# Seven block products for the second input half of the second feed-forward parts

## The reference

```python
def swiglu(x, w_in, w_out):                     # w_in 1024 x 5632, w_out 2816 x 1024
    gate, up = jnp.split(x @ w_in, 2, axis=-1)
    return (jax.nn.silu(gate) * up) @ w_out
x = x + 0.5 * swiglu(rmsnorm(x, p['ffn2_norm'][i]), p['ffn2_w_in'][i], p['ffn2_w_out'][i])
```

## Time and profile before

| | us |
|---|---|
| median of 3 runs (2357.9 to 2358.71) | 2358.68 |
| profiled execution, span from first to last instruction | 2357.9 |
| PE busy | 2332.7 (99%) |
| DVE busy | 1295.9 (55%) |
| ACT busy | 869.0 (37%) |
| POOL busy | 609.4 (26%) |

### The profile page before, as it was taken

The page is one execution under the profiler, slowest core; times in us unless marked ns, Lnnn a source line. Parts: engine busy times, 40 slices in busy tenths (PEclk is TensorE's granted clock), DMA queues, the critical chain, the costliest instruction groups (busy, mean ns, idle before and its releaser), DMA issues.

```text
span 2357.9 us, 50146 instructions
## 1 busy us (share of the span) xinstructions
PE 2332.7 (99%) x21043; PEld 2270.3 (96%) x21043; DVE 1295.9 (55%) x1906; ACT 869.0 (37%) x1399; POOL 609.4 (26%) x591
## 2 busy tenths in 40 slices
PE   8999999999999999999999999999999999999999
PEld 8999999889979999999999999999999979999999
DVE  6653643964576443445543344577777666443443
ACT  4422333453233321322433233267775233321323
POOL 4779967331103000004111010432122102000003
PEclk9999999999999999999999999999999999999999
DMA  6455445553562333333543333233332653333332
GB/s 167 128 161 149 123 134 169 171 170 107 166 242 84 98 99 91 96 96 99 158 117 111 100 108 115 83 100 108 104 111 77 213 188 91 97 94 94 98 94 94
DMA packets 483707, 289.19 MB, mean 123 GB/s; under 512 B 22289, under 2 KB 466962, under 8 KB 482514
## 3 DMA queue, kind: packets, MB, share of 16 engines
q1 hardware_dynamic: 477856, 280.66, 40.4%
q0 software_dynamic: 560, 1.84, 0.6%
q10 hardware_dynamic: 5122, 4.25, 0.5%
HBM read 258.86 MB, written 27.85 MB: 122 GB/s over the span
## 4 chain that ended last, share of the span: by engine, by line
PE 90%; DVE 4%; POOL 2%; ACT 1%; issue 1%; DMA 1%; SPq 0%; DVEq 0%; POOLq 0%; ACTq 0%
PE lin L3021 51%; PE lin L3026 25%; PE mis L2512 4%; POOL sTmp L737 1%; PE mis L2650 1%; PE lin L2600 1%; PE lin L2762 1%; PE mis L2633 1%; PE lin L2757 1%; PE lin L2983 1%; POOL sGe L738 0%; DVE w_lo L1827 0%; POOL sFe L738 0%; PE lin L2650 0%; PE mis L2626 0%
## 5 line engine op out<-in xcount | busy, mean ns | idle before, releaser
L1827 DVE TENSOR_TENSOR w_lo<-raw,w_hi 128x1024 fp32r<-128x1024 f32 (+1 forms) x322 | 464.0, 1441 | 294.4 <-ACT w_hi L1330 293.7
L1330 ACT ACTIVATE w_hi<-raw 128x1024 fp32r<-128x1024 f32 (+1 forms) x328 | 365.1, 1113 | 314.2 <-PE lin L3026 244.4
L3021 PE MATMUL lin<-a_rear,w_hi 128*128 128x264 f32 x3552 | 455.6, 279 | 0.0
L3021 PE MATMUL lin<-a_front,w_hi 128*128 128x256 f32 x3552 | 451.5, 279 | 1.1 <-DVE a_rear L1840 0.7
L3021 PEld LDWEIGHTS lin<-a_rear,w_hi 128*128 128x128 f32 x3552 | 432.6, 188 | 0.0
L3021 PEld LDWEIGHTS lin<-a_front,w_hi 128*128 128x128 f32 x3552 | 424.4, 188 | 4.5 <-issue 1.8
L3026 PE MATMUL lin<-a_rear,w_lo 128*128 128x264 f32 x1776 | 245.1, 278 | 0.0
L3026 PE MATMUL lin<-a_front,w_lo 128*128 128x256 f32 x1776 | 240.5, 277 | 1.0 <-DVE w_lo L1827 1.0
L2391 DVE SCALAR_TENSOR_TENSOR xT<-lin,xT 128x520 f32<-128x520 f32 (+1 forms) x87 | 60.9, 700 | 322.8 <-PE lin L3026 322.1
L1063 POOL TENSOR_TENSOR acc<-xT 128x520 f32<-128x520 f32 x8 | 12.2, 1521 | 864.6 <-DVE xT L2391 836.6
L3026 PEld LDWEIGHTS lin<-a_rear,w_lo 128*128 128x128 f32 x1776 | 223.8, 188 | 0.0
(11 more groups left out here) (512 smaller groups left out, 3181.5 us busy)
## 6 DMA issues: line engine op xcount, KB each, us to landing
raw<-in_ffn_w_in_dram SPq DMA_DIRECT2D x176, 512.0 KB, 3.9
raw<-in_ffn_w_out_dram SPq DMA_DIRECT2D x64, 704.0 KB, 4.6
kc<-in_cache_mem_k_dram SPq DMA_DIRECT2D x32, 512.0 KB, 7.1
vc<-in_cache_mem_v_dram SPq DMA_DIRECT2D x16, 1024.0 KB, 9.1
raw<-in_hg_w_in_dram SPq DMA_DIRECT2D x32, 512.0 KB, 4.3
raw<-in_xattn_w_kv_dram SPq DMA_DIRECT2D x16, 512.0 KB, 4.4
raw<-in_s_w_glu_dram SPq DMA_DIRECT2D x16, 512.0 KB, 4.0
raw<-in_xattn_w_q_dram SPq DMA_DIRECT2D x16, 512.0 KB, 3.9
```

Of the source, the lines that this page charges most:

```text
L1330: act.activation(w_hi[:, j, 0:kt, :], raw[:, j, 0:kt, :], ACT.Copy).then_inc(hi_ready, 1)
L1827: dve.tensor_tensor(low_weights(n, j), raw[:, j, 0:kt, :], w_hi[:, j, 0:kt, :].bitcast(F32), ALU.subtract).then_inc(lo_ready, 1)
L3021: pe.matmul(lpart(j, half), high[:, k, :], (x_lo if u else x_hi)[half][:, k, :], start=start and u == 0 and k == 0, stop=False)
```

## The change

`ffn2_in1` of both layers (2 x 11 pairs) is computed by Winograd's form of Strassen's scheme. The 2x2 blocks are: weights A11, A12 (gate, tiles 0 to 3 and 4 to 7 of the contraction), A21, A22 (value); tokens B11, B21 (the first 260 tokens, tiles 0 to 3 and 4 to 7), B12, B22 (the last 260). Per pair there are seven products P1 to P7 of 4 tiles x 3 matmuls with 260 columns, 84 matmuls:

- P1 = A11 B11, P2 = A12 B21, P4 = A22 T4, P6 = S2 T2, P5 = S1 T1, P7 = S3 T3, P3 = S4 B22, in this order on PE, each in a PSUM bank of its own.
- S1 = A21+A22, S2 = S1-A11, S3 = A11-A21, S4 = A12-S2, four sums of 128x512 per pair on DVE (`weight_sums`); their high parts on ACT (`high_sums`, two of 128x1024), their low parts on POOL (`low_sums`, two of 128x1024, of which the first waits for S4 too).
- Normalised token blocks and T1 to T4 (four steps of eight DVE ops with 260 columns, `mixed`), their high parts on ACT and low parts on DVE (128x1820 each), made in `ffn2_in0`, which is now unrolled.
- The results are put together on DVE from PSUM and `rows` (`with_p2_p6`, `with_p5_p7`, `with_p3_p4`), then silu, product and split as before.

SP's code is unchanged, but in `ffn2_in1` `lo_ready` is raised only by `low_22`, by 2; the low part of the gate's weights raises `first_low`. At the end of `ffn2_out0` DVE makes the first pair's sums before it adds the last tile to x. Two hgrn semaphores are merged, and `rows_in` shrinks from 8 to 4 semaphores.

```diff
+    COMBOS = {"B11": 0, "B22": 1, "B21": 2, "T1": 3, "T2": 4, "T3": 5, "T4": 6}
...
+    SUMS = {"S1": 0, "S2": 1, "S3": 2, "S4": 3}
...
+    MIX_RAW = {("ffn2_in0", l, 1 + 2 * k): k for l in range(DEPTH) for k in range(KQ)}
+    MIX_SPLIT = {("ffn2_in0", l, 2 + 2 * k): k for l in range(DEPTH) for k in range(KQ)}
...
+            def low_sums(layer):
+                for q in range(FH * layer, FH * (layer + 1)):
+                    pool.wait_ge(combined, of_weights(q, 1))
+                    for pair in range(2):
+                        pool.wait_ge(combined_high, of_weights(q, pair))
+                        blocks = slice(2 * pair, 2 * pair + 2)
+                        pool.tensor_tensor(sum_lo[:, q % FH % 2, blocks], sum_raw[:, q % FH % 2, blocks],
+                                           sum_hi[:, q % FH % 2, blocks].bitcast(F32), ALU.subtract).then_inc(combined_low, 1)
...
+                def high_22(p):
+                    act.wait_ge(raw_arrived[1], 16 * (p + 1))
+                    act.wait_ge(chunk_done, 2 * p0)
+                    wait(act, product_done, 4 * (FH * layer + p - p0 - 1) + 2)
+                    act.activation(w_hi[:, 1, KQ:KD, :], raw[:, 1, KQ:KD, :], ACT.Copy).then_inc(hi_ready, 1)
+                def high_sums(q, pair):
+                    act.wait_ge(combined, of_weights(q, pair))
+                    blocks = slice(2 * pair, 2 * pair + 2)
+                    act.activation(sum_hi[:, q % FH % 2, blocks], sum_raw[:, q % FH % 2, blocks], ACT.Copy)\
+                        .then_inc(combined_high, 1)
...
+                for i in range(FH):
+                    p, q, more = p0 + i, FH * layer + i, i + 1 < FH
+                    if i == 0:
+                        high_sums(q, 0)
+                        high_22(p)
+                        high_sums(q, 1)
+                    else:
+                        gate(i - 1)
+                    act.wait_ge(product_done, 4 * q + 1)
+                    act.activation(rows[:, ROW_P1], bank_p1, ACT.Copy).then_inc(product_kept, 1)
+                    if more:
+                        high_sums(q + 1, 0)
+                    split(p + 1, 0, n if more else n + 1)
+                    if i:
+                        hidden_hi(i - 1)
+                    if more:
+                        high_22(p + 1)
+                        high_sums(q + 1, 1)
...
+            def weight_sums(p, q, pair):
+                for j in range(2):
+                    dve.wait_ge(raw_arrived[j], 16 * (p + 1))
+                s = {name: sum_raw[:, q % FH % 2, b] for name, b in SUMS.items()}
+                w = {f"A{j + 1}{e + 1}": raw[:, j, KQ * e:KQ * (e + 1), :] for j in range(2) for e in range(2)}
+                if pair == 0:
+                    step.link(dve.tensor_tensor(s["S1"], w["A21"], w["A22"], ALU.add))
+                    dve.tensor_tensor(s["S2"], s["S1"], w["A11"], ALU.subtract).then_inc(combined, 1)
+                else:
+                    dve.tensor_tensor(s["S3"], w["A11"], w["A21"], ALU.subtract)
+                    dve.wait_ge(combined, of_weights(q, 0))
+                    dve.tensor_tensor(s["S4"], w["A12"], s["S2"], ALU.subtract).then_inc(combined, 1)
...
                                 split_part(p + 1, slice(0, FREE_LOW)).then_inc(lo_part, 1)
+                                if seven(n + 1):
+                                    weight_sums(p + 1, FH * layer, 0)
+                                    weight_sums(p + 1, FH * layer, 1)
...
+                            if last and j == 1 and seven(n + 1):
+                                split_part(p + 1, slice(FREE_LOW, KD)).then_inc(first_low, 1)
...
+                def low_11(p):
+                    dve.wait_ge(hi_ready, 2 * p + 1)
+                    dve.tensor_tensor(w_lo8[:, 0], raw[:, 0, 0:KD, :], w_hi[:, 0, 0:KD, :].bitcast(F32),
+                                      ALU.subtract).then_inc(first_low, 1)
+                def low_22(p):
+                    dve.wait_ge(hi_ready, 2 * p + 2)
+                    dve.tensor_tensor(w_lo8[:, 1, KQ:KD, :], raw[:, 1, KQ:KD, :], w_hi[:, 1, KQ:KD, :].bitcast(F32),
+                                      ALU.subtract).then_inc(lo_ready, 2)
...
+                def with_p2_p6(q):
+                    dve.wait_ge(product_done, 4 * q + 3)
+                    dve.wait_ge(product_kept, q + 1)
+                    return step.mark(dve.tensor_tensor(rows[:, ROW_GATE.stop - 1:ROW_U2 + 1:ROW_U2 - ROW_GATE.stop + 1],
+                                                       banks_p2_p6, twice(ROW_P1), ALU.add))
+                def with_p5_p7(q, u2):
+                    dve.wait_ge(product_done, 4 * q + 4)
+                    step.after(u2)
+                    step.link(dve.tensor_tensor(rows[:, ROW_V:ROW_U3 + 1], banks_p5_p7, twice(ROW_U2), ALU.add))
+                    dve.tensor_tensor(rows[:, ROW_VALUE.start], bank_p5, rows[:, ROW_U3], ALU.add)
+                def with_p3_p4(p):
+                    dve.wait_ge(chunk_done, 2 * p + 2)
+                    dve.tensor_tensor(rows[:, ROW_GATE.start:ROW_VALUE.stop:ROW_VALUE.stop - 1 - ROW_GATE.start], banks_p3_p4,
+                                      rows[:, ROW_V:ROW_U3 + 1], ALU.add).then_inc(used[0], 1)
...
+                for i in range(FH):
+                    p, q, more = p0 + i, FH * layer + i, i + 1 < FH
+                    if i == 0:
+                        low_22(p)
+                    else:
+                        with_p3_p4(p - 1)
+                    if more:
+                        weight_sums(p + 1, q + 1, 0)
+                    if i:
+                        gated(i - 1)
+                    if more:
+                        weight_sums(p + 1, q + 1, 1)
+                        low_11(p + 1)
+                    u2 = with_p2_p6(q)
+                    if more:
+                        low_22(p + 1)
+                    else:
+                        split(p + 1, 0, n + 1)
+                    if i:
+                        hidden_lo(i - 1)
+                    with_p5_p7(q, u2)
+                with_p3_p4(p)
+                gated(FH - 1)
+                hidden_lo(FH - 1)
...
+                def high(bank, w, block):
+                    for x in (mix_hi, mix_lo):
+                        for k in range(KQ):
+                            pe.matmul(bank, w[:, k, :], x[:, COMBOS[block], k, :],
+                                      start=x is mix_hi and k == 0, stop=False)
+                def low(bank, w, block):
+                    for k in range(KQ):
+                        ins = pe.matmul(bank, w[:, k, :], mix_hi[:, COMBOS[block], k, :], start=False,
+                                        stop=k == KQ - 1)
+                    return ins
+                pe.wait_ge(combined_low, of_tokens(layer, KQ - 1))
+                for i in range(FH):
+                    p, q = p0 + i, FH * layer + i
+                    a1_hi, a1_lo = w_hi[:, 0], w_lo8[:, 0]
+                    s_hi, s_lo = ({name: t[:, i % 2, b] for name, b in SUMS.items()} for t in (sum_hi, sum_lo))
+                    pe.wait_ge(hi_ready, 2 * p + 1)
+                    wait(pe, product_kept, q)
+                    high(bank_p1, a1_hi[:, 0:KQ], "B11")
+                    if i == 0:
+                        pe.wait_ge(lo_part, LOW_PARTS.index(n) + 1)
+                    else:
+                        pe.wait_ge(first_low, q + 1)
+                    low(bank_p1, a1_lo[:, 0:KQ], "B11").then_inc(product_done, 1)
+                    if i:
+                        pe.wait_ge(lo_ready, 2 * p + 2)
+                    pe.wait_ge(used[0], p - 1)
+                    high(bank_p2, a1_hi[:, KQ:KD], "B21")
+                    if i == 0:
+                        pe.wait_ge(first_low, q + 1)
+                    low(bank_p2, a1_lo[:, KQ:KD], "B21").then_inc(chunk_done, 1)
...
+                    pe.wait_ge(hi_ready, 2 * p + 2)
+                    pe.wait_ge(used[0], p)
+                    high(bank_p4, w_hi[:, 1, KQ:KD], "T4")
+                    pe.wait_ge(lo_ready, 2 * p + 2)
+                    low(bank_p4, w_lo8[:, 1, KQ:KD], "T4").then_inc(product_done, 1)
+                    pe.wait_ge(combined_high, of_weights(q, 0))
+                    high(bank_p6, s_hi["S2"], "T2")
+                    pe.wait_ge(combined_low, of_weights(q, 0))
+                    low(bank_p6, s_lo["S2"], "T2").then_inc(product_done, 1)
```

More of the change, by code:

```diff
@@ L55, in link, with mark, after @@
         self.eng.wait_ge(self.sem, self.off + self.n)
+    def mark(self, ins):
+        ins.then_inc(self.sem, 1)
+        self.n += 1
+        return self.off + self.n
+    def after(self, mark):
+        self.eng.wait_ge(self.sem, mark)
     def loop(self, i, first, per):
@@ L451, in trunk_kernel @@
     hg = {name: sem("hg_" + name) for name in
-          ("fill", "void_dve", "void_act", "lb_diff", "lb_exp", "lb", "consts", "log", "decay", "exps", "scaled_pool",
```

(63 more changed lines are left out.)

70 lines of the change are left out of this document (64 added, 6 removed).

## The result

The changed kernel takes **2460.7 us** (median of 4 runs, 2458.55 to 2461.67) against 2358.55 of the kernel before (4 runs on the same chip). That is 1.0431 times, 95% interval 1.0416 to 1.0446. The forecast was 2459. The profiled execution took 2460.23, its span is 2458.5. The page after, answering to the earlier trace rows: engines' busy time, the granted clock in 40 slices, the chain that ended last.

What follows compares the result with a forecast made beforehand. PE bounds the kernel before (99% busy); a closed loop of loads, DVE and POOL would bound the changed stretches: 4.9+10x15.7+9.4 = 171.3 us against 121.7, so 2357.9+99+2 = 2459 us, range 2380 to 2480.

Steps and rivals of the forecast that it cites:

- PE would no longer bound: Changed stretches: a pair's 84 matmuls need 9.66 us, but the loop sets the turn; PE busy near 60%.
- The loop: ffn2_in1, low_22 through both loads, sums and low_11 to the next low_22: 12.0 us a turn alone; as rival 2386, chance 0.11.
- The port, POOL first: SBUF port shared with DVE: POOL's low part starts about 0.1 us before low_11, turn 15.7 us; chance 0.52.
- the other order: Rival at the port: low_11 goes before POOL, turn 13.5 us, 2421 us; chance 0.25 including turns of both kinds.
- Entry: Start of each changed stretch: first low_22 ends at 943.05, 4.9 us after PE's start.
- The last pair: End of each changed stretch: P2, then P4 after with_p3_p4, then five products of 1.38, 9.4 us.
- P6's slack: PE in a turn: P6 has 7 us of slack, so a clock fall for part of a pair costs nothing.
- clock rival: PE in the changed stretches: lower clock throughout, 19.3 us a pair, two stretches +182, 2541 us; chance 0.05.
- The first input half: ffn2_in0, unrolled with added DVE and ACT work: +2 us, ends 0 and +8.
- The faster rival: Changed stretches: loads overlap enough that PE bounds at 9.66 us a pair, 2330 us; chance 0.07.
- 14.3+10T: Time of one changed stretch, T being one turn of the loop; breaks even with 121.7 us at T = 10.7.

Runs made afterwards that it cites:

- run 2: Changed kernel with POOL's low parts of the sums cut to 8 of 1024 columns from each layer's third pair, part of the computation left out: 2390.28 us.
- run 3: Changed kernel with both low parts of the sums made on DVE behind low_22 instead of on POOL: 2387.32 us.
- Run 4: As run 3, but SP loads raw[:,0] once low_11 has read it, not low_22: 2370.77 us.
- Run 1: Changed kernel with POOL's first low part of a pair's sums let go only behind low_11: 2427.6 us.
- Run 10: Order of run 8, with POOL's low part held until the moved hidden_lo is done: 2343.84 us, 0.993 of the kernel before.
- run 8: Version with DVE's sums, low_11, low_22 first and POOL keeping one low part; hidden_lo of the pair before moved behind low_22: 2371.63 us.

## Why the prediction was right

- **PE would no longer bound**: 84 matmuls a pair and a stretch of 172.05 us, PE busy 135 of it, 78% where the forecast had near 60%. At 119 ns the 924 matmuls are 110 us, 64%. The rest is mostly the lower clock: PE was busy 10.77 us in the turn from 1020.41, with a granted clock of 0.99, and 13.20 in that from 958.02, with 0.81.
- **The loop.** Forecast 12.0 us without POOL; 11.85 in run 2, 11.82 in run 3. The 5.7 us of the two loads came out as 0.6+5.1. Run 4 took one release out of the loop and 16.6 us out of the time.
- **The port, POOL first.** Forecast 15.7 a turn; 15.49 on average (`low_22` ends at 942.89 in the first turn and at 1097.81 ten turns later). POOL started 0.07 us after S4's end, not 0.15, so its lead over `low_11` was 0.18 instead of 0.1. Run 1 showed what hung on it: forecast 13.5 and 2421 for the other order, measured 13.75 and 2427.6.
- **Entry**: forecast 4.9 us from PE's start to the end of `low_22`, measured 4.67 (938.22 to 942.89) and 4.61.
- **The last pair was mis-sized**: forecast 9.4 us, measured 12.46 (1097.81 to 1110.27) and 12.35. PE's two products behind the wait, P2 and P4, ran at the lower clock. PE's rows, then the window that holds them:

```profile
1097.86 2.10 PE L3202 MATMUL lin<-mix,w_hi 128*128 128x260 f32 x8 [2.02 <-DVE w_lo L2587]
...
1100.63 1.94 PE L3202 MATMUL mis<-mix,w_hi 128*128 128x260 f32 x8
...
1103.23 1.45 PE L3202 MATMUL lin<-mix,sum 128*128 128x260 f32 x8
...
1107.84 1.12 PE L3202 MATMUL mis<-mix,sum 128*128 128x260 f32 x8
...
1110.27 1.97 PE L3325 MATMUL lin<-f_front,w_hi 128*128 128x256 f32 x15 [0.84 <-issue]
```

```profile
1097.86:1103.23 5.37, 5.37 (x25) 5.37 (x25) 2.97 (x6) 1.10 (x3) 0.00 (x0) 0.50 0.80 221
```

  The two products took 5.37 us instead of 2.86. Not all of that is lost, since P4 has to wait for `with_p3_p4` anyway: in the turn at nearly the full clock it started 2.50 us behind `low_22` (1022.91), here 2.82. The clock costs these 0.3 us, 1.2 in P4 (2.60 instead of 1.43) and 0.3 in P6 (1.76 instead of 1.43), 1.8 together. About 1.0 more lies between the last product and the next stream, 2.43 us from start to start instead of 1.43. PE stands idle there for 0.84 us in every version, where the kernel before has no gap; no run shows why. The last 0.2 is 119 ns a matmul instead of 115. The prediction had the clock as a rival for whole stretches and called its falls free because of P6's slack; in the last pair there is none. The gap at the end was no term of its sum. Over the ten turns the 0.2 us that each came out short gives most of this back: 4.67+154.92+12.46 is 172.05, forecast 171.3.
- **The clock in the turns.** The granted clock was between 0.78 and 0.93 in 19 of the 20 turns and 0.99 in one. So PE fell to the lower level in nearly every turn, as the prediction's clock rival described it, and not once only as in the earlier trace rows. It did not lengthen the turns: that with 0.99 took 15.50 us, one with 0.80 took 15.30.
- **The first input half**: forecast +2, measured about 0. From the end of the first stretch to the start of the second it is 1104.88 us, against 1104.85 before.
- **The faster rival** was added up wrongly. By its own 14.3+10T a stretch at T = 9.66 is 110.9 us, which makes 2336 and not 2330. No other number rests on it. Run 10, with PE as the bound, has stretches of 113.7 and 114.6.
- The mechanism was right, but that the time is right to 0.1% is luck: errors of 2 to 6 us cancel, +6 for the two last pairs, -4 for the turns, -2 for the first half.

## What to carry to other kernels

When a change shares or drops a release of a buffer, write down the closed loop from that release back to itself (issue, landing, each operation in the engine's own order) and compare its length with what the bounding engine needs for the same step. Here it is 12 us against the 11.07 of before and PE's new 10.0, and the versions that did better (11.15, 10.07, 10.0) all took something out of that loop. Before moving work to an idle POOL, look at which DVE operations with two SBUF inputs run beside it: here its 2.4 us were free beside operations that read PSUM, and cost 1.5 to 2.2 us beside the others, even for an operation of 0.4 us. A faster order can bring the two together by accident, as run 8 did.
